# Attention stage of a diffusion backbone: finer waits of the first scores, two modulation panels ahead of the softmax units, modulation rows copied a unit later, two weight remainders on GpSimd

## What is computed

```python
mod_l = split((silu(c) @ mod_w[i] + mod_b[i]), 6)          # six vectors of 1024 per layer
z = h @ w_in; q = rmsnorm(z_q) @ w_uq; kv = rmsnorm(z_kv) @ w_ukv    # 8 heads, 128 + 64 rotary
s_ctx = qn @ kc_nope.T + q_rope @ kc_rope.T
s_lat = qn @ kl_nope.T + rotated(q_rope) @ rotated(kl_rope).T
p = softmax(concat(s_ctx, s_lat) / sqrt(192))
o = (p[..., :C] @ v_ctx + p[..., C:] @ v_lat) @ w_o        # context queries see context keys only
```

## Time and profile before

| | |
|---|---|
| median of 3 runs | 2323.53 us (2320.32, 2323.53, 2325.91) |
| profiled execution, its own time | 2329.59 us |
| span of its trace | 2327.8 us |
| TensorE busy | 2134.6 us, 92% |
| VectorE busy | 1152.3 us, 50% |
| ScalarE busy | 865.2 us, 37% |
| GpSimd busy | 120.5 us, 5% |
| mean granted clock of TensorE | 0.944 |

### The profile page before, as it was taken

How to read it: one execution, slowest core, us unless ns; L and a number is a source line. 1 busy time by engine, 2 the same in 40 slices (tenths; PEclk the granted TensorE clock), 3 DMA queues, 4 the chain that set the end, 5 groups by cost and what they waited for, 6 DMA issues and landing times.

```text
span 2327.8 us, 31537 instructions
## 1 busy us (share of the span) xinstructions
PE 2134.6 (92%) x13233; PEld 1660.7 (71%) x13233; DVE 1152.3 (50%) x1941; ACT 865.2 (37%) x1416; POOL 120.5 (5%) x185
## 2 busy tenths in 40 slices
PE   4999989899999989998989999999648899988998
PEld 2656556687777767755547777886647799977997
DVE  2322453645556556644344654754392545446454
ACT  2442123533333353221234333334532544525444
POOL 0000000102101200010001110011000000000000
PEclk8999799999999999999999999999558999999999
DMA  6335242445544555433044563334632365424553
GB/s 246 127 113 172 86 142 76 129 152 159 175 152 155 190 177 184 176 122 110 26 155 164 171 216 132 125 130 167 230 145 82 122 195 181 128 84 145 181 181 109
DMA packets 228683, 344.23 MB, mean 148 GB/s; under 512 B 9238, under 2 KB 192321, under 8 KB 226300
## 3 DMA queue, kind: packets, MB, share of 16 engines
q1 hardware_dynamic: 218016, 313.41, 39.4%
q0 software_dynamic: 9808, 28.53, 4.1%
q10 hardware_dynamic: 716, 0.26, 0.0%
HBM read 319.76 MB, written 26.61 MB: 149 GB/s over the span
## 4 chain that ended last, share of the span: by engine, by line
PE 82%; DVE 10%; ACT 4%; DMA 2%; issue 1%; SPq 1%; POOL 0%; ACTq 0%; DVEq 0%
PE bank L953 20%; PE bank L954 19%; PE bank L955 19%; PE bank L397 4%; PE bank L819 4%; PE bank L864 2%; ACT arena L691 2%; PE bank L1705 1%; PE bank L2405 1%; PE bank L1341 1%; DVE arena L720 1%; DVE h_lo L724 1%; DMA arena<-mod_w 1%; ACT h_hi L695 1%; PE bank L637 1%
## 5 line engine op out<-in xcount | busy, mean ns | idle before, releaser
L953 PE MATMUL bank<-h_hi,w_hi 128*128 128x512 f32 (+1 forms) x1480 | 516.0, 349 | 23.2 <-DVE h_lo L724 22.3
L954 PE MATMUL bank<-h_lo,w_hi 128*128 128x512 f32 (+1 forms) x1480 | 506.5, 342 | 0.0
L955 PE MATMUL bank<-h_hi,w_lo 128*128 128x512 f32 (+1 forms) x1480 | 506.4, 342 | 0.0
L915 DVE TENSOR_TENSOR w_lo<-ring,w_hi 128x1024 fp32r<-128x1024 f32 (+1 forms) x282 | 323.4, 1185 | 305.1 <-ACT w_hi L910 305.0
L953 PEld LDWEIGHTS bank<-h_hi,w_hi 128*128 128x128 f32 x1480 | 284.0, 192 | 68.6 <-DVE h_lo L724 31.6
L910 ACT ACTIVATE w_hi<-ring 128x1024 fp32r<-128x1024 f32 (+1 forms) x282 | 274.4, 1018 | 93.7 <-PE bank L955 93.2
L955 PEld LDWEIGHTS bank<-h_hi,w_lo 128*128 128x128 f32 x1480 | 283.8, 192 | 32.7 <-issue 0.4
L954 PEld LDWEIGHTS bank<-h_lo,w_hi 128*128 128x128 f32 x1480 | 284.4, 192 | 29.4 <-issue 0.4
L953 PE MATMUL bank<-g_hi,w_hi 128*128 128x512 f32 (+1 forms) x704 | 241.3, 343 | 0.0
L954 PE MATMUL bank<-g_lo,w_hi 128*128 128x512 f32 (+1 forms) x704 | 237.0, 337 | 0.0
L955 PE MATMUL bank<-g_hi,w_lo 128*128 128x512 f32 (+1 forms) x704 | 236.7, 336 | 0.0
(11 more groups left out here) (322 smaller groups left out, 2942.2 us busy)
## 6 DMA issues: line engine op xcount, KB each, us to landing
ring<-ffn_w SPq DMA_DIRECT2D x120, 1024.0 KB, 5.1
mod_ring<-mod_w SPq DMA_DIRECT2D x88, 1024.0 KB, 7.1
ring<-ffn_w SPq DMA_DIRECT2D x16, 768.0 KB, 4.6
ring<-hy_w_in SPq DMA_DIRECT2D x12, 1024.0 KB, 5.3
arena<-mod_w SPq DMA_DIRECT2D x8, 1024.0 KB, 17.0
s_in_weights<-arena POOLq DMA_DIRECT2D x32, 256.0 KB, 3.1
s_out_weights<-arena POOLq DMA_DIRECT2D x16, 512.0 KB, 4.7
ring<-s_w_glu SPq DMA_DIRECT2D x8, 1024.0 KB, 5.7
```

The source lines that it names most:

```text
L915: nc.vector.tensor_tensor(self.lo[:, i % SPLIT, a:b], self.w.slot(i)[:, a:b], self.hi[:, i % SPLIT, a:b].bitcast(F32), ALU.subtract).then_ ...
L953: nc.tensor.matmul(o, w[0], v[0], start=first, stop=False)
L954: nc.tensor.matmul(o, w[0], v[1], start=False, stop=False)
L955: return nc.tensor.matmul(o, w[1], v[0], start=False, stop=last)
```

## The change

Five edits, all in layer 0's attention:

- The first three scores wait each for what they read and for the bank that they write, no longer for the last rotation: unit 0 for `q_moved` 13 and the rotation of head 0, unit 1 for `q_moved` 14, unit 2 for `rot` 8. Scores(0) is issued ahead of the last `turn_rope`. Values(0), which writes the bank that the last rotation reads, waits for `rot` 9.
- The panels of units 1 and 3 move into a new place, "start", between scores(2) and weigh(0), and the turn of the vector completed by the eighth head's panel goes with them. The other ten panels keep their units, and the refills their order in the queue.
- On ScalarE the copy of modulation rows of unit u is issued in unit u + 1, after the exponentials and the output of that unit; on VectorE the modulation end of unit u is issued at the end of unit u + 1.
- The four half-panel remainders of `wo[0]` are made by GpSimd, each waiting for its rounding on ScalarE.
- VectorE waits, after its last unit, until `wo[0]` is split, before it begins with `wo[1]`.

```diff
--- before.py
+++ after.py
@@ -909,10 +909,10 @@
                 a, b = self.halves(i)[j]
                 nc.scalar.activation(self.hi[:, i % SPLIT, a:b], self.w.slot(i)[:, a:b], ACT.Copy).then_inc(w_rounded, 1)
 
-            def remain(self, dve, i, j):
+            def remain(self, dve, i, j, unit=nc.vector):
                 a, b = self.halves(i)[j]
                 dve.wait_ge(w_rounded, 2 * (self.s0 + i) + j + 1)
-                nc.vector.tensor_tensor(self.lo[:, i % SPLIT, a:b], self.w.slot(i)[:, a:b], self.hi[:, i % SPLIT, a:b].bitcast(F32),
+                unit.tensor_tensor(self.lo[:, i % SPLIT, a:b], self.w.slot(i)[:, a:b], self.hi[:, i % SPLIT, a:b].bitcast(F32),
                                         ALU.subtract).then_inc(w_split_ready, 1)
 
             def ahead(self, step, eng, i=None):
@@ -1221,8 +1221,9 @@
                     mods.place((self, "in", n), n in (1, 3, 5, 7), self.win.w.p0 + self.panel[n] + 5)
                 for hd in range(HEADS):
                     mods.place((self, "q", hd), 1, min(self.wuq.w.p0 + hd + 5, self.wo[1].w.p0))
+                mods.place((self, "start"), 2, self.wo[1].w.p0)
                 for u in range(len(self.units)):
-                    mods.place((self, "unit", u), u % 2 if u < 24 else 0, self.wo[1].w.p0)
+                    mods.place((self, "unit", u), u % 2 if 4 <= u < 24 else 0, self.wo[1].w.p0)
 
             def gpsimd(self, pool):
 
@@ -1230,6 +1231,9 @@
                 pool.wait_ge(mod_used, MOD_EARLY)
                 pool.dma_start(self.tab[0:ROPE], A["k_rope"]).then_inc(self.loaded, 16)
                 pool.dma_start(self.turn[0:ROPE], A["k_turn"]).then_inc(self.loaded, 16)
+                for i in range(2):
+                    for half in range(2):
+                        self.wo[0].remain(pool, i, half, nc.gpsimd)
 
             def tensor(self, pe):
                 lead_in(pe, self.win, self.pre, [(0, 0, bank[0][:, :]), (0, 1, bank[1][:, :]), (1, 0, bank[2][0:ROPE, :])], self.z_summed)
@@ -1302,15 +1306,16 @@
                     if part:
                         mods.tensor(pe, (self, "q", hd))
                         self.turn_rope(pe, hd)
-                pe.wait_ge(self.q_moved, 16)
-                self.turn_rope(pe, HEADS)
 
                 def scores(u):
                     hd, qb, k0, nk = self.units[u]
                     if u < self.AHEAD:
-                        pe.wait_ge(self.rot, 9)
+
+                        pe.wait_ge(*((self.q_moved, 13), (self.q_moved, 14), (self.rot, HEADS))[u])
                     else:
                         pe.wait_ge(self.exped, u - self.AHEAD + 1)
+                    if qb < 2:
+                        pe.wait_ge(self.rot, hd + 2)
                     b = self.score_bank(u)
                     q = slice(qb * P, (qb + 1) * P)
                     if qb < 2:
@@ -1337,13 +1342,19 @@
                     pe.wait_ge(self.p_moved, u + 1)
                     if u:
                         pe.wait_ge(self.o_split, u)
+                    else:
+                        pe.wait_ge(self.rot, HEADS + 1)
                     for j in range(nk):
                         last = nc.tensor.matmul(self.HEAD_OUT, self.v[:, k0 // P + j, hd * P:(hd + 1) * P],
                                                 self.pt[:, u % 2, j * P:(j + 1) * P], start=(j == 0), stop=(j == nk - 1))
                     last.then_inc(self.o_summed, 1)
                 n = len(self.units)
-                for u in range(self.AHEAD):
-                    scores(u)
+                scores(0)
+                pe.wait_ge(self.q_moved, 16)
+                self.turn_rope(pe, HEADS)
+                scores(1)
+                scores(2)
+                mods.tensor(pe, (self, "start"))
                 for u in range(n):
                     weigh(u)
                     if u + self.AHEAD < n:
@@ -1430,7 +1441,6 @@
                         self.wuq.ahead(self.wuq.round, act, hd)
                         mods.scalar(act, (self, "q", hd))
                 scale = float((NOPE + ROPE) ** -0.5)
-
                 def out(u):
                     hd, qb, k0, nk = self.units[u]
                     act.wait_ge(self.o_summed, u + 1)
@@ -1442,11 +1452,15 @@
                         act.wait_ge(self.p_turned, u - 1)
                     nc.scalar.activation(self.e[:, u % 2, 0:nk * P], self.score_bank(u)[:, 0:nk * P], ACT.Exp, bias=self.mx[:, u % 2:u % 2 + 1],
                                          scale=scale, accum_out=self.sm[:, u % 2:u % 2 + 1]).then_inc(self.exped, 1)
+                    if u == 0:
+                        mods.scalar(act, (self, "start"))
                     if u >= 2:
                         out(u - 2)
-                    mods.scalar(act, (self, "unit", u))
+                    if u:
+                        mods.scalar(act, (self, "unit", u - 1))
                     if u in self.WO_AT:
                         self.wo[0].round(act, *divmod(self.WO_AT.index(u), 2))
+                mods.scalar(act, (self, "unit", len(self.units) - 1))
                 out(len(self.units) - 2)
                 out(len(self.units) - 1)
                 self.wo[1].ahead(self.wo[1].round, act)
@@ -1513,11 +1527,11 @@
                         peak(u + 2)
                     dve.wait_ge(self.p_turned, u + 1)
                     nc.vector.tensor_copy(self.pt[:, u % 2, 0:nk * P], bank[2 + u % 2][:, 0:nk * P]).then_inc(self.p_moved, 1)
-                    mods.vector(dve, (self, "unit", u))
-                    if u in self.WO_AT:
-                        self.wo[0].remain(dve, *divmod(self.WO_AT.index(u), 2))
+                    mods.vector(dve, (self, "unit", u - 1) if u else (self, "start"))
+                mods.vector(dve, (self, "unit", n - 1))
                 remainder(n - 2)
                 remainder(n - 1)
+                dve.wait_ge(w_split_ready, self.wo[0].nth_split(1, 1))
                 self.wo[1].ahead(self.wo[1].remain, dve)
                 for c in range(KD - 1):
                     self.post.cross(dve, c)
```

## The result

| | before | after |
|---|---|---|
| median | 2322.49 us (4 runs, 2320.32 to 2325.91) | 2301.52 us (4 runs, 2301.03 to 2301.75) |
| profiled execution, own time | 2329.59 us | 2301.03 us |
| span of its trace | 2327.8 us | 2299.2 us |
| mean granted clock | 0.944 | 0.953 |

The changed kernel takes 0.9908 of the time of before, interval 0.9891 to 0.9925: faster by 21.0 us, where 28.8 us were forecast. The time lies inside the range of 2288 to 2306 us, but 1.5 us past the forecast's own range of 2288 to 2300 and nearer to rival B's 2303.9 than to the forecast's 2294.7. Two things stand out at once. And the four runs of the changed kernel lie within 0.7 us of each other, those of before within 5.6.

The account below looks back on a forecast made before the run. TensorE, 82% of the span, bounds the kernel, so its waits and clock falls count. 12.5 + 17.3 - 1.0 = 28.8 us off the median 2323.53 gives 2294.7 us; own range 2288 to 2300, 8 in 10 2288 to 2306.

Parts of the forecast that it names:

- rival B: Scaling stands behind each GpSimd instruction, costing 4.6 us, and clock falls at units 9 and 17: 2303.9 us; chance 0.16.
- the prediction's own signs of being wrong: L1508 beginning only as GpSimd ended, the grant falling inside the units, or the stage after attention losing the units' gain.
- Term 1: Start of attention: earlier first scores and full clock bring unit 2 to 244.5 instead of 257.0, gaining 12.5 us.
- Rival A: Clock falls at the first scores all the same; start gains 2.6 instead of 12.5 us, time 2304.6; chance 0.16.
- Term 2: Units 2 to 25: waits vanish or shrink, taking the units from 97.0 to 79.7 us, gaining 17.3 us.
- I take each row down to 13.1: Units 2 to 25: each four-unit row priced at the clean 13.1 us of units 2 to 5, plus what remains.
- the 0.7 of units 9 and 17: TensorE still waits 0.7 us in units 9 and 17, behind the copy and rounding on ScalarE.
- Term 3: Remainders on GpSimd holding up VectorE's scaling: 1.0 us lost, between 0 and 4.6.
- the row is nearer to nothing: Remainders on GpSimd: profile row of VectorE's L1804 at 2.28 us beside GpSimd, as L1803 alone, suggests little slowing of VectorE.

Follow-up runs that it names:

- old start: Changed kernel with the first three scores waiting for the last rotation and two panels back in units 1 and 3: 2304.01 us, in a later job 2309.85 us.
- the rows alone: Kernel before with only the modulation rows moved a unit later, remainders on VectorE: 2303.22 us, ratio 0.9909.
- the second profile: Kernel before, unedited, profiled once more: median 2322.36 us, ratio 1.0006, span 2321.3 us.
- the remainders on VectorE: Changed kernel with the four remainders of the output weights back on VectorE in units 8, 12, 16, 20: 2297.31 us, ratio 0.9893.
- the quarters: Changed kernel with each of GpSimd's four instructions cut into four pieces: 2295.66 us, ratio 0.9872.
- the later version: Changed kernel with rounding and remainder two units later, in units 10, 14, 18, 22, remainders on GpSimd: 2294.92 us, ratio 0.9870.
- the start alone: Kernel before with only finer waits and two panels ahead of unit 0's transposes; rows in their own unit, remainders on VectorE: 2316.57 us, ratio 0.9977.
- the panels alone: Changed kernel with the first scores waiting for the last rotation again, two panels still ahead of unit 0's transposes: 2309.36 us, ratio 0.9939.
- the waits alone: Changed kernel with the finer waits kept but the two panels back in units 1 and 3: 2299.06 us, ratio 0.9907.

## Why the prediction was right or wrong

**Right: direction, range, the place and the way.** TensorE's waits and its clock in this stage were what could be gained. Counted from the last head's panel, unit 2 came 0.4 us later than worked out, and of the waits the three behind the rows' copy vanished. Two of the prediction's own signs of being wrong came too, in part: the scalings ended just behind GpSimd's instructions, and the grant fell once inside the units (0.90 in units 14 to 17).

**Term 1, 12.5 us: right for the execution it was read from, too large for the median.** The profile of before and that of after differ by 12.1 us here. But the same old start reached unit 2 after 16.8 us in the one profile in which its clock held, against 15.7 with the new one, so the term is about 1 us where it held. Where it fell, unit 2 came after 27.8 and 27.7 us in the two profiles of before, but after 23.8 and 23.9 us where the rows were already a unit later (the old start again, the rows alone). So the term is 12 us on the kernel before and 8 with the rows moved: the two edits seem to overlap by 4 us, which the sum of the terms leaves out. Two profiles of each kind are too few to call that certain. What the old start adds in the medians is 2.5 us in one job and 8.3 in the other over the changed kernel's 2301.5. Rival A had the idea from the wrong side: it asked whether the new start might lose its clock, which it did at the start in none of eight profiles, and not how often the old one keeps it.

**Term 2, 17.3 us: the mechanism right, the base too high.** The step that failed is "I take each row down to 13.1": the rows were one execution's, and 2.8 us of the 20.4 in units 6 to 9 was a fall of the clock that the second profile does not have. With the remainders on VectorE the rows after are 12.5, 14.3, 14.1, 14.3, 14.1 and 12.2 us, against the forecast 12.6, 14.2, 13.1, 14.2, 13.1 and 12.5; so the waits were worked out well, the 0.7 of units 9 and 17 too, except that L915 on VectorE still costs units 13 and 21 their 0.8. In medians, taken over jobs, the rows alone bring 19.3 us, the start on top of them 5.9, and GpSimd takes 4.2 of that back: 21.0.

**Term 3, 1.0 us: mis-sized, and the wrong end taken.** The forecast took "the row is nearer to nothing", from a VectorE instruction that ran undisturbed beside GpSimd's. That one had begun first. A scaling that comes second took 1.82, 1.55, 1.81 and 1.55 us in place of 0.49, and the waits of units 9, 13, 17 and 21 were 1.66, 0.74, 1.65 and 0.74 us, 4.8 together. Without the hold 1.4 were to be left, which is what the quarters show (0.72 and 0.71), so term 3 measured 3.4 us, between the forecast's 1.0 and rival B's 4.6. In the medians the edit costs 4.2 us against the remainders on VectorE. Rival B is thus what happened in the trace, with one fall of the clock behind it instead of two, and its time of 2303.9 was nearer than the forecast's. The Trainium skill (GPSIMD Engine Reference, Key points) says that GpSimd contends for SBUF interfaces with VectorE instructions in a 2-port mode or with two SBUF inputs. These rows agree if the scaling, which reads one tensor of SBUF and writes SBUF, runs in such a mode; the trace does not show the mode. Not all that VectorE does is held: the copy out of PSUM beside GpSimd's instruction (L1529 in the later version, above) took 0.42 us, no more than elsewhere.

**The sum against the median.** The forecast took the whole difference, made on an execution of 2329.59 us, off a median of 2323.5. Of the 57 runs between 2314.1 and 2333.4 us only four lay above that execution. The part of its time that was bad luck could not be gained by the median execution. The 2300.8 us that the same sum gives on the profiled execution lie within 0.7 us of the result, but only because two things cancel: the stage gave 24.5 us of the 28.8 (12.1 for term 1, 12.4 for terms 2 and 3), and 4.0 us that the change does not account for came from ahead of it and behind it. The right base was a bound from both sides for each fall of the clock: held, or lost.

## What to carry to other kernels

Where a profile shows waits that the clock answers by falling, price each twice, with and without the fall, and take a second profile before pricing: the same program may show either. An edit that removes such a wait gains the wait surely and the fall only in the share of executions that have it, and it also narrows the spread. Work moved to GpSimd is not free because nobody waits for GpSimd: look which VectorE instruction falls beside it and whether that one is on the path, and if so put GpSimd's work where TensorE has work of its own for longer, or cut it into pieces.

## What the runs showed of the hardware

- A VectorE scaling from SBUF to SBUF that begins while GpSimd has a tensor by tensor instruction of 128x1024 under way ends just after that instruction does: 0.3 us after it for 128x512 (265.43 + 1.82 against 264.61 + 2.35), 0.15 for 128x256 (270.71 + 1.89 against 270.11 + 2.34). With GpSimd's work in four instructions it took 0.88 us and ended before GpSimd was through. GpSimd's own time, 2.35 us, is the same as alone, 2.34.
- Two idle microseconds of TensorE ahead of the first scores were followed by half clock in five of six profiles and not in the sixth; the waits of units 8 and 9, 1.9 and 2.21 us, by half clock in one profile of before and in that of the start alone, and not in the other of before. Of the ten waits of 1.65 or 1.66 us in five profiles (units 9 and 17 of the changed kernel, of both with the old start, of the panels alone and of the waits alone) five were followed by a fall and five not. In the profiles without a wait over 0.9 us in the units (remainders on VectorE, later or in quarters, rows alone) the clock did not fall in the units. The Trainium skill (TensorE: Matmul & The Clock Gate, Part 1) says that the gate runs free of the kernel, so that the same program meets it at different points; the two profiles with the old start agree, 1.00 and 0.50 in the same stretch. The two were also 0.7 us apart when the last head's panel began (228.29 and 228.97); that nothing else differed between them is argued, not shown.
- Once at half speed TensorE stayed there for 14 to 24 us at the old start, although it was busy nearly all the time, and only some 3 to 14 us in the other falls of the stage. Why the first scores leave it there longer was not tried.
